# A mixture layer of a backbone: from half of the tiles dense to all but one

## The reference

```python
def block(ub):                                    # 128 tokens
    q = (ub @ P['peer_wq']).reshape(t, 8, 2, 128)
    s = jnp.einsum('thpd,pkd->thpk', q, P['peer_subkeys'])
    sv, si = lax.top_k(s, 16)                     # per head and half
    cand = (sv[:, :, 0, :, None] + sv[:, :, 1, None, :]).reshape(t, 8, 256)
    top, ci = lax.top_k(cand, 16)
    e = take(si[:, :, 0], ci // 16) * 128 + take(si[:, :, 1], ci % 16)
    gate = jax.nn.softmax(top, axis=-1)
    act = gelu(jnp.einsum('tkd,td->tk', P['peer_u'][e], ub))    # 128 picks a token
    return jnp.einsum('tk,tkd->td', gate * act, P['peer_v'][e])
```

## Time and profile before

| | us |
|---|---|
| Median of three runs (6656.40 to 6680.77) | 6679.44 |
| The profiled execution | 6678.65 |
| its span, first to last instruction | 6676.6 |
| PE busy | 5486.7 |
| DVE busy | 3833.7 |
| POOL busy | 1875.6 |
| ACT busy | 1192.3 |
| granted clock of TensorE, mean | 0.856 |

### The profile page before, as it was taken

One profiled execution on the slowest core, in us unless ns is written; L12 is line 12 of the kernel. 1 busy time (PEld: TensorE's weight loads), 2 busy tenths in 40 slices (PEclk: granted clock), 3 DMA queues, 4 the chain that ended last, 5 costly groups with the idle time before them and its releaser, 6 DMA issues.

```text
span 6676.6 us, 62677 instructions
## 1 busy us (share of the span) xinstructions
PE 5486.7 (82%) x22755; PEld 3635.5 (54%) x22755; DVE 3833.7 (57%) x8953; ACT 1192.3 (18%) x2559; POOL 1875.6 (28%) x1700
## 2 busy tenths in 40 slices
PE   8899877868757779999997899887786668788876
PEld 3699454735554334554552489744655555455554
DVE  1554163737267898876674355342737376766555
ACT  1100032221373000000002110021312450000001
POOL 0000000000487564554551000000001584444442
PEclk9899978778856889999998889899567768898988
DMA  6000101012115999999995200001012249999996
GB/s 210 14 1 1 38 1 32 1 32 63 64 76 238 387 397 389 387 392 358 387 389 206 86 1 1 13 26 32 1 32 64 79 173 374 349 367 369 359 347 245
DMA packets 290066, 1165.07 MB, mean 175 GB/s; under 512 B 24416, under 2 KB 106592, under 8 KB 205024
## 3 DMA queue, kind: packets, MB, share of 16 engines
q0 software_dynamic: 92160, 671.13, 24.9%
q1 hardware_dynamic: 192272, 441.96, 18.9%
q10 hardware_dynamic: 5328, 47.99, 1.7%
HBM read 1116.94 MB, written 44.04 MB: 174 GB/s over the span
## 4 chain that ended last, share of the span: by engine, by line
PE 63%; DMA 13%; DVE 13%; ACT 5%; issue 4%; POOL 1%; ACTq 0%; DVEq 0%; SPq 0%; POOLq 0%
PE psum L413 63%; DMA weight_ring<-in_ut 12%; DVE arena L1261 3%; ACT y_features L975 2%; ACT arena L903 2%; DVE arena L1540 1%; DVE arena L1615 1%; DVE arena L1270 1%; DVE arena L1264 1%; DVE u_features L1267 1%; DVE x_tokens L1261 1%; DVE arena L1382 1%; DVE arena L1267 0%; ACT y_features L977 0%; DVE arena L1357 0%
## 5 line engine op out<-in xcount | busy, mean ns | idle before, releaser
L413 PE MATMUL psum<-u_features,weight_ring 128*128 128x256 f32 (+2 forms) x6464 | 2014.4, 471 | 345.3 <-DMA weight_ring<-in_ut 313.8
L413 PEld LDWEIGHTS psum<-u_features,weight_ring 128*128 128x128 f32 x6464 | 1312.0, 205 | 1074.3 <-DMA weight_ring<-in_ut 361.8
L413 PE MATMUL psum<-weight_ring,consts 128*128 128x512 f32 x2560 | 1141.8, 593 | 2.6 <-DMA weight_ring<-in_uv 1.9
L413 PE MATMUL psum<-arena 128*128 128x64 f32 (+5 forms) x7136 | 983.5, 320 | 45.5 <-DVE arena L1540 23.9
L413 PEld LDWEIGHTS psum<-arena 128*128 128x128 f32 (+2 forms) x7136 | 842.1, 218 | 131.2 <-issue 32.1
L1248 POOL DMA_INDIRECT arena<-in_uv,arena x560 | 833.4, 1488 | 160.4 <-POOL arena L1244 87.2
L413 PEld LDWEIGHTS psum<-weight_ring,consts 128*128 128x128 f32 x2560 | 484.8, 190 | 540.6 <-issue 491.2
L1762 DVE SCALAR_TENSOR_TENSOR y_features<-arena,y_features 128x1024 f32<-128x1024 f32 x560 | 718.0, 1282 | 12.0
L1747 DVE CUSTOM_DVE_ANT_0 arena<-arena,y_features 128x1024 f32<-128x1024 f32 x560 | 665.1, 1219 | 36.7 <-DMA arena<-in_uv,arena 36.6
L1244 POOL TENSOR_TENSOR arena<-consts 128x1 f32<-128x1 f32 x320 | 343.4, 1073 | 1148.5 <-DVE y_features L1762 1125.9
L1230 POOL TENSOR_SCALAR y_features<-consts 128x128 f32<-128x128 f32 x640 | 525.8, 838 | 463.1 <-ACT consts L965 267.7
(11 more groups left out here) (194 smaller groups left out, 5123.1 us busy)
## 6 DMA issues: line engine op xcount, KB each, us to landing
weight_ring<-in_ut SPq DMA_DIRECT2D x256, 512.0 KB, 8.8
weight_ring<-in_uv SPq DMA_DIRECT2D x256, 512.0 KB, 8.6
weight_ring<-in_ws SPq DMA_DIRECT2D x234, 512.0 KB, 3.6
gate_blocks<-arena ACTq DMA_DIRECT2D x20, 2048.0 KB, 6.3
consts<-gate_blocks SPq DMA_DIRECT2D x16, 768.0 KB, 17.3
arena<-gate_blocks SPq DMA_DIRECT2D x16, 768.0 KB, 18.3
arena<-in_uv,arena POOLq DMA_INDIRECT x560, 10.4
consts<-gate_blocks SPq DMA_DIRECT2D x16, 512.0 KB, 15.5
```

What stands on the lines that cost most here:

```text
L413: return pe.matmul(o, w, x, start=first, stop=last, skip_group_check=True)
```

## The change

- In the first layer five tiles are dense and one (tile 0) gathers; in the second three are dense and one (tile 2) gathers. `PASSES` says which dense tiles share a pass over the tables: the first layer reads the tables twice, for tiles 4, 5 and then for tiles 1, 2, 3 (256 blocks); the second once, for tiles 3, 4, 5 (128 blocks).
- The front makes the gates of the first pass alone. Tiles 1, 2 and 3 of the first layer are routed by DVE between the blocks of pass 0, two steps a block, and PE does one gate group between an up and a down block; a planner (`plans`) fixes the blocks: groups of tile 1 at blocks 25 to 56, of tile 2 at 58 to 89, of tile 3 at 91 to 122.
- One slot of the gathered tile goes with a block: in the first layer from block 126 on (the second pass), in the second from block 0 on.
- Between the passes ACT copies the two finished tiles out of PSUM (`results_kept`). The first matmul of a bank starts its sum, so the six zeroing matmuls go.
- The tables' blocks have four buffers a table instead of two; the gathers five instead of eight.
- `find` searches for two heads at a time, and one one-column instruction stands ahead of two or four searches; the searches don't wait for each other.
- Gate groups begin behind piece 5 (first layer) and piece 11 (second layer) of part 1. Part 0 has 256 columns in the first layer and 384 in the second, part 1 has 512 and 128. Gate groups use two PSUM banks instead of three.

```diff
-GSLOTS = 8
-GROUP = 2
-RING = GSLOTS // GROUP
-GROUPS = TOPK // GROUP
+GSLOTS = 5
 BLOCKS = EXPERTS // P
 QUAD = 4
 QUARTER = 32
-BLOCKS_A_HEAD = ((4, 6, 6), (8, 8))
+GROUPS = P // QUAD
+PASSES = (((4, 5), (1, 2, 3)), ((3, 4, 5),))
+GATHERED = (0, 2)
+PICKS = HEADS * TOPK
+STAGES = 9
+PARTS = HEADS // 2 * STAGES + 8
+TURN_AT = (4, 10)
+FIRST_SLOT = (126, 0)
...
-        UP = [WR[:, i * D:(i + 1) * D] for i in range(2)]
-        DOWN = [WR[:, (2 + i) * D:(3 + i) * D] for i in range(2)]
...
+        UP = [WR[:, 0:D], WR[:, D:2 * D], SC[0][:, 0:D], SC[0][:, D:2 * D]]
+        DOWN = [WR[:, 2 * D:3 * D], WR[:, 3 * D:4 * D], SC[1][:, 0:D], SC[1][:, D:2 * D]]
...
-            ts = tiles(l)
-            return ts[len(ts) // 2:]
...
+            return [t for ts in PASSES[l] for t in ts]
...
+        plans = []
+        for l in range(DEPTH):
+            plan = {n: {} for n in ("route", "exp", "turn", "group", "slot")}
+            free, when = 0, 0
+            for d in range(len(PASSES[l][0]), len(dense_tiles(l))):
+                for part in range(PARTS):
+                    if part == PARTS - 1:
+                        when = (free + 1) // 2 * 2 + 2
+                        free = when
+                    plan["route"].setdefault(free // 2, []).append((dense_tiles(l)[d], part))
+                    free += 1
+                ready = free // 2 + 1
+                plan["exp"][ready - 2] = dense_tiles(l)[d]
+                first = max(ready + 1, max(plan["group"], default=-2) + 2)
+                plan["turn"][first - 1] = d
+                for q in range(GROUPS):
+                    plan["group"][first + q] = d * GROUPS + q
+            for i in range(PICKS):
+                plan["slot"].setdefault(FIRST_SLOT[l] + i * (blocks(l) - 4 - FIRST_SLOT[l]) // PICKS, []).append(i)
+            plans.append(plan)
         block = ctx.enter_context(nc.Block())
...
-                def load_up(e):
-                    if e >= 2:
-                        sp.wait_ge(*at("hidden", l, e - 2))
-                    sp.dma_start(UP[e % 2], a["ut"][l * BLOCKS + e]).then_inc(up_in[e % 2], 16)
-                def load_down(e):
-                    if e >= 2:
-                        sp.wait_ge(*at("block added", l, e - 2))
-                    r = l * EXPERTS + e * P
-                    sp.dma_start(DOWN[e % 2], a["uv"][r:r + P, D:2 * D]).then_inc(down_in[e % 2], 16)
+                def load_up(m):
+                    n = blocks_before(l) + m
+                    if m >= 4:
+                        sp.wait_ge(*at("hidden", l, m - 4))
+                    sp.dma_start(UP[n % 4], a["ut"][l * BLOCKS + m % BLOCKS]).then_inc(up_in[n % 4], 16)
+                def load_down(m):
+                    n = blocks_before(l) + m
+                    if m >= 4:
+                        sp.wait_ge(*at("block added", l, m - 4))
+                    r = l * EXPERTS + m % BLOCKS * P
...
+            def down_block(l, m):
+                n, e = blocks_before(l) + m, m % BLOCKS
+                pe.wait_ge(down_in[n % 4], 16 * (n // 4 + 1))
+                pe.wait_ge(*at("block weighted", l, m))
+                if e == 0 and m:
+                    pe.wait_ge(*at("results kept", l))
+                    pe.wait_ge(*at("gates evicted", l, len(dense_tiles(l)) * GROUPS - 1))
+                for i in range(len(block_tiles(l, m))):
                     for j in range(2):
-                        ins = mm(bank(2 * m + j), HID[e % 2][:, m * P:(m + 1) * P], DOWN[e % 2][:, j * 512:(j + 1) * 512],
-                                 False, False)
-                hidden(ins, "block added", l, e)
+                        ins = mm(bank(2 * i + j), HID[m % 4][:, i * P:(i + 1) * P], DOWN[n % 4][:, j * 512:(j + 1) * 512],
+                                 e == 0, e == BLOCKS - 1)
+                hidden(ins, "block added", l, m)
...
-                for m in range(1, len(dense_tiles(l))):
-                    turn_picks(l, m)
-                    for q in range(P // QUAD):
-                        gate_block(l, m, q)
+                for k in range(early, len(PASSES[l][0]) * GROUPS):
+                    if k % GROUPS == 0:
+                        turn_picks(l, k // GROUPS)
+                    gate_block(l, k)
...
-                for b in range(2 * len(dense_tiles(l))):
-                    mm(bank(b), cf(K_ZERO)[0:1, :], CF[0:1, 0:512], True, False)
...
-                pe.wait_ge(*at("block activated", l, BLOCKS - 1))
+                pe.wait_ge(*at("gates evicted", l, len(PASSES[l][0]) * GROUPS - 1))
+                for m in range(2):
+                    up_block(l, m)
+                for m in range(blocks(l)):
+                    if m + 2 < blocks(l):
+                        up_block(l, m + 2)
+                    if m in plans[l]["turn"]:
+                        turn_picks(l, plans[l]["turn"][m])
+                    if m in plans[l]["group"]:
+                        gate_block(l, plans[l]["group"][m])
+                    down_block(l, m)
...
+                plan = plans[l]
+                for m in range(blocks(l)):
+                    if m == BLOCKS + 2:
+                        results_kept(l)
+                    block_activated(l, m)
...
+                    if m not in plan["group"] and m - 1 in plan["group"]:
+                        gates_evicted(l, plan["group"][m - 1])
+                    if m in plan["exp"]:
+                        gate_weights(l, plan["exp"][m])
+                    if m in plan["turn"]:
+                        picks_kept(l, plan["turn"][m])
+                    if m in plan["group"]:
+                        gate_group(l, plan["group"][m])
+                    for s in plan["slot"].get(m, []):
+                        slot_weight(l, s)
...
+                pool.wait_ge(*at("routed", l, dense_tiles(l)[-1]))
+                pool.wait_ge(*at("placed", l, GATHERED[l], 1))
+                for s in range(PICKS):
+                    b, n = slot_at(l, s)
+                    if s >= GSLOTS:
+                        pool.wait_ge(*at("slot summed", l, s - GSLOTS))
+                    done(pool.tensor_tensor(DUM, ident[:, 0:1], ident[:, 0:1], ALU.mult))
+                    pool.indirect_dma_start(GB[b], None, a["uv"], IndirectOffsetOnAxis(ap=IDX[:, s:s + 1], axis=0))\
+                        .then_inc(rows_in[b], 16)
...
+            def pause():
+                dve.wait_ge(SEM["routing_steps"], route.n)
+                dve.tensor_tensor(DUM_DVE, ident[:, 0:1], ident[:, 0:1], ALU.mult)
+            def link(ins, *name):
+                route(ins, *name)
+                dve.wait_ge(SEM["routing_steps"], route.n)
...
+            def find(l, t, pair, stage):
+                sc, lists = score_buffer(l, t), []
+                for h in (2 * pair, 2 * pair + 1):
+                    for j in range(2):
+                        c = (4 * j + h % 4) * 16
+                        lists.append((sc[:, (2 * h + j) * P:(2 * h + j + 1) * P], SV[:, c:c + 16], SI[:, c:c + 16]))
+                grids = [(CAND[n], TOP[:, (2 * pair + n) * 16:(2 * pair + n + 1) * 16],
+                          CI[:, (2 * pair + n) % 4 * 16:(2 * pair + n) % 4 * 16 + 16]) for n in range(2)]
+                if stage == 5:
+                    dve.wait_ge(SEM["routing_steps"], route.n)
+                    for n in range(2):
+                        route(dve.tensor_tensor(split(CAND[n], 16), spread(lists[2 * n][1], 16), rep(lists[2 * n + 1][1], 16), ALU.add))
+                pause()
+                half = 8 * (stage in (3, 4, 7, 8))
+                for s, values, places in lists if stage < 5 else grids:
+                    if stage in (0, 3, 5, 7):
+                        route(dve.max(values[:, half:half + 8], s))
+                    if stage in (1, 4, 6, 8):
+                        route(dve.max_index(places[:, half:half + 8], values[:, half:half + 8], s))
+                if stage in (2, 6):
+                    if stage == 6:
+                        pause()
+                    for s, values, places in lists if stage < 5 else grids:
+                        route(dve.match_replace(s, values[:, 0:8], s, -3.0e38))
...
+                plan = plans[l]
+                for m in range(blocks(l)):
+                    block_weighted(l, m)
+                    for t, part in plan["route"].get(m, []):
+                        route_part(l, t, part)
+                    for s in plan["slot"].get(m, []):
+                        slot_dot(l, s)
+                        if s:
+                            slot_summed(l, s - 1)
+                slot_summed(l, PICKS - 1)
```

519 lines of the change are left out of this document (221 added, 298 removed).

## The result

The changed kernel takes 7571.59 us (median of four, 7566.34 to 7576.11), the kernel before in the same runs 6680.1 (6656.4 to 6687.43): a ratio of 1.134 [1.131, 1.137]; the brackets hold the 95% interval, here and below. The forecast was 7618 with a range of 7560 to 7730. The profiled execution took 7572.0, its span is 7570.1. Of experiment 9's ten runs two, of 10859.9 and 14477.0 us, fell in a slower state of the chip and are left out.

The account below looks back on a forecast made before the run. It took PE's matmuls, not the transfers, to bound the loops. Layer 0 adds 707 us (834-120-7) and layer 1 232 (153+82-3), together 939 on 6678.65: 7618 us, range 7560 to 7730.

Parts of the forecast that it names:

- The block loops: Both layers' loops: layer 0 takes 2279 us, 834 more than before; layer 1 takes 1308, 153 more.
- The step that carried the case: Block loops: 10.31 us a three-tile block and 6.88 a two-tile block are the matmuls' own price, not the transfers'.
- the group's 0.89 us: Pass 0 of layer 0: each of 96 gate groups adds 0.89 us of matmuls, 85 in all.
- the ring: Table loads: blocks land in 8.8 us and have four buffers over three blocks of time, so layer 1's waits go.
- layer 0's 141 us beyond its matmuls: Layer 0's loop before: 1444.8 us, 1304 of them matmuls, the rest waits for tables at its beginning.
- DMA was to be near 0.4 in both passes: Layer 0's two passes: DMA share near 0.4, with tables at 152 GB/s and 203.
- Layer 0's front: Layer 0, first query piece to POOL's last sides: some 437 us, before 557.
- The first turn: Layer 0's front: first turn of picks after five pieces and four scores, at 1626 with the first piece at 1523.6.
- the ten groups left over and the last scores: Layer 0's front, after the cycles: ten groups at 3.3 us and 3 us for the last scores.
- The cycle of 16.9 us: Layer 0's front: eleven cycles of a 512-column piece with two groups, 16.9 us each, 186 in all.
- Layer 1's front: Layer 1, first query piece to POOL's end: 481 us, before 399, so 82 more.
- The handover: POOL's end to the first down block: 29 us in both layers (25 to 36), 7 and 3 less than before.

Follow-up runs that it names:

- experiment 9: The kernel before with six gather buffers instead of eight and nothing else changed: 6648.0 us against 6657.99, ratio 0.998.
- experiment 5: The kernel before with its gathers left out but for the first eight of each layer: 6333.83 us (one run).
- Experiment 2: The changed kernel with one matmul instead of four in each gate group of pass 0: 7502.78 us (one run).
- Experiment 1: The changed kernel with two buffers a table instead of four: 7574.57 us, ratio 1.135 against 1.134.
- experiment 4: The changed kernel with all gate groups behind the last query piece in both layers: 7545.77 us, ratio 1.131.
- experiment 3: The changed kernel with layer 1's gathers begun two blocks later: 7560.49 us, ratio 1.133.

## Why the prediction was right, and where it was off

**The block loops** (2279 and 1308 forecast, 2277.6 and 1306.8 found). The step that carried the case held: 10.31 and 6.88 us are the matmuls' own price. Its reason was that a piece of the same columns takes as long where DMA is three quarters idle, and experiment 5 shows the same for the blocks themselves in layer 1. Experiment 2 shows the group's 0.89 us as columns. Experiment 1 shows that inside the passes the waits for tables would have gone with two buffers too: the gathers' going did that, and not the ring, as I had put beside it. The ring saves the three waits at the starts of the passes. Two readings beside the sum were off. I had put layer 0's 141 us beyond its matmuls down to waits for tables; experiment 5 shows that some 80 of them stay without the gathers and are DVE's. And DMA was to be near 0.4 in both passes and was 0.57 and 0.65, at 187 and 225 GB/s where I had 152 and 203: I had left out the gates' own loads and stores, and the share doesn't follow the rate (0.95 stood at 371).

**Layer 0's front** (437, 436.0). The agreement to 1 us is partly luck. The first turn came 107.2 us behind the first piece, 4.8 later than reckoned. PE waited 3.51 us for DVE, but DVE wasn't late; by its own row it had waited for ACT:

```profile
1621.97 0.28 DVE L1481 TENSOR_REDUCE arena<-arena 128x8 f32<-128x128 f32 x1 [17.10 <-ACT arena L989]
```

DVE had the tile's sums 89 us behind the first piece. ACT's exponential (L989) stands in its program behind the evictions of piece 5 and its scores, and the turn hangs on it. The other way, the ten groups left over and the last scores took 31.7 us (1807.84 to 1839.53) and not 36, because POOL had two groups more in hand. The cycle of 16.9 us is 1737.74-1720.82 = 16.92 and held. In it a piece takes 8.78 us where the same piece takes 7.03 in the free run. Over 1700 to 1760 us the mean granted clock is 0.78, between its two levels; in the free run of experiment 4 (1640 to 1700) it is 1.00, the upper one. The Trainium skill, "TensorE: Matmul & The Clock Gate", section "A second HAM failure mode: psum-queue depth-cycling", says that bursts parted by micro-idles lose throughput to the clock; in the cycles the trace agrees, and in pass 0, where lanes and sides lie ready, it never starts: 650 us at 1.00 with a group in nearly each block.

**Layer 1's front** (481, 464.5) is the largest miss, three terms of one sign. The turn came 5850.40-5731.76 = 118.6 us behind the first piece, not 123. Five cycles took 10.1 each, not 11.2. And what was left of the first tile took 69.7 us (5901.97 to 5971.66) where I had 22 groups at 3.3 and a turn, 76: POOL had 12 groups behind it when the cycles ended, and made the other 20 at 3.23. These are 4, 5 and 6 us. The two whole tiles behind it were right, 224.6 for 225.6. The lines of PE for a cycle and of POOL for the groups alone (they answer to the earlier trace rows; 128 rows of POOL are a tile, 80 are 20 groups):

```profile
5850.40 0.90 PE L522 MATMUL psum<-consts 128*128 128x128 f32 x3 [3.03 <-DVE consts L1300]
...
5871.18 3.01 PE L441 MATMUL psum<-u_features,weight_ring 128*128 128x128 f32 x16
...
5881.25 3.09 PE L441 MATMUL psum<-u_features,weight_ring 128*128 128x128 f32 x16
```

```profile
5907.12 64.54 POOL L1275 TENSOR_SCALAR y_features<-consts 128x128 f32<-128x128 f32 x80 [1.25 <-PE psum L441]
5978.01 106.10 POOL L1275 TENSOR_SCALAR y_features<-consts 128x128 f32<-128x128 f32 x128 [6.35 <-ACT consts L996]
6090.46 105.80 POOL L1275 TENSOR_SCALAR y_features<-consts 128x128 f32<-128x128 f32 x128 [6.34 <-ACT consts L996]
```

**The handover**, from POOL's end to the first down block (29 each, 15.9 and 27.1). I took the 36.4 and 32.2 us of before and shortened them by the table wait alone. PE's rows of that place in layer 0, before and after:

```profile
2083.81 10.58 PE L413 MATMUL psum<-consts 1*128 1x512 f32 x12 [0.84 <-ACT arena L903]
2094.32 12.23 PE L413 MATMUL psum<-u_features,weight_ring 128*128 128x384 f32 x32
2110.27 7.12 PE L413 MATMUL psum<-u_features,weight_ring 128*128 128x384 f32 x16 [3.73 <-DMA weight_ring<-in_ut]
```

```profile
1954.62 8.96 PE L441 MATMUL psum<-u_features,weight_ring 128*128 128x256 f32 x32 [0.80 <-ACT arena L934]
1963.42 3.62 PE L441 MATMUL psum<-u_features,arena 128*128 128x256 f32 x16
1967.61 3.67 PE L441 MATMUL psum<-weight_ring,arena 128*128 128x512 f32 x8 [0.58 <-DVE arena L1507]
```

Before, the first down block followed the third up at once, so PE's own matmuls and one wait for a table block set the 36.4, and not the gates. Its terms tell where the 20.5 us went: the six zeroing matmuls of the first row, 10.5; the three up blocks, 256 columns wide instead of 384, 19.2 to 12.4; the table wait, 3.7; and 0.58 us of waiting for gates came in. I had left the first two out. That the gates now don't stop PE for longer needs their load of 4.1 us with no gather beside it; one of 13.9 us, as in layer 1, would as an estimate have put the first down block some 26 us behind POOL's end. In layer 1 the number agrees and its parts don't: the zeroing went (7.1), three wider up blocks cost 3.9 more, and PE's wait for ACT of 7.7 became one for gates of 5.78, which experiment 3 takes away (20.6).

**What stays open.** The start to the first piece was 7.9 us shorter, in instructions that the change doesn't touch. It isn't chance: in all five profiled versions of the changed kernel it is 1515.7 to 1517.8, in all seven of the kernel before 1522.6 to 1525.6. The cause wasn't looked for. Not tried was a version that has its gathers in layer 1 before POOL's last groups.

## What to carry to other kernels

Before work moves from one engine to another, price it in the receiving engine's own unit: here a gathered tile's transfers cost the loops 68 us and a dense tile 440 us of columns, and here no hiding of waits could pay that back. A DMA share of 0.93 beside waits for its data isn't yet a full memory path; a deeper ring is a cheap test of it. In this case the path was full when a load asked for earlier only made another one late, at the same GB/s. A forecast that is right in the total can be right by terms that cancel, and so can an experiment: compare stage by stage. Serial groups that wait for an engine cost more laced between the pieces of both fronts here than behind them; in pass 0, where their operands lie ready a block earlier, they cost only their columns.

## What the runs showed of the hardware

- With two buffers a table the transfers of layer 1's loop moved 362 GB/s at a share of 0.94, with four 407 at 1.02, though the indirect gathers were the same; over the whole run the median landing time of the first table's blocks rose from 8.8 to 13.4 and 16.2 us. Depth bought throughput and cost latency.
- The first load of gates, 512 KB in layer 0 and 768 KB in layer 1, landed in 4.1 us with no gather beside it, and in 13.9 us with five that were started up to 10 us ahead; 5.1 in layer 1 when the five were held back. In the kernel before, where it was asked for 1 us ahead of the first gather, 768 KB landed in 5.2 us, and the next load, asked for 0.4 us later, in 14.1. Table blocks of 512 KB land in 3.5 us in the version without gathers and in 8.8 with them.
- The same piece of 512 columns took 7.03 us in a free run and 8.78 between groups, at a mean granted clock of 1.00 and 0.78. Between the loops some 1500 equal matmul records took PE 328 us at 0.68 and 296 at 0.73, in two kernels that are the same there.
